# Block 1's causal attention: four projections as three fp32r products each

## The reference

```python
k, v = split(modulate(x, kv_shift, kv_scale) @ w_kv)          # 256x1024 @ 1024x2048
q = (modulate(x, shift, scale) @ wq) * 64 ** -0.5             # 16 heads of 64
s = q @ k.T - slope[h] * (t - pos), masked where pos > t
y = (softmax(s) @ v) @ wo                                     # 256x1024 @ 1024x1024
x = layer_norm(ALPHA * x + gate * y)
```

## Time and profile before

| | |
|---|---|
| Runs (us) | 2406.71, 2400.88, 2400.84; median 2400.88 |
| Profiled execution | 2402.46 us, span 2400.6 us |
| TensorE busy | 2268.5 us (94% of the span) |
| VectorE, ScalarE, GpSimd busy | 1248.1, 952.3, 113.6 us |
| DMA | 535.63 MB, 223 GB/s on average |

### The profile page before, as it was taken

How to read it: one execution, slowest core, us unless ns; L and a number is a source line. 1 busy time by engine, 2 the same in 40 slices (tenths; PEclk the granted TensorE clock), 3 DMA queues, 4 the chain that set the end, 5 groups by cost and what they waited for, 6 DMA issues and landing times.

```text
span 2400.6 us, 33267 instructions
## 1 busy us (share of the span) xinstructions
PE 2268.5 (94%) x12878; PEld 1739.5 (72%) x12878; DVE 1248.1 (52%) x2279; ACT 952.3 (40%) x1702; POOL 113.6 (5%) x96
## 2 busy tenths in 40 slices
PE   5999999998999899889999899999999998899999
PEld 3877774544576454368888689888888796698887
DVE  4724544111333411167746556777677636666776
ACT  2532212110322211165444664645545446645543
POOL 1000000000000000000024100000000052000000
PEclk8999999999999999989999899999999999999999
DMA  9966468999614899946644325466566534154663
GB/s 347 320 231 234 158 262 376 429 429 422 252 71 171 376 429 429 400 139 194 196 151 158 106 76 198 137 205 183 158 198 194 171 109 174 36 189 128 211 184 96
DMA packets 310253, 535.63 MB, mean 223 GB/s; under 512 B 14894, under 2 KB 200944, under 8 KB 296304
## 3 DMA queue, kind: packets, MB, share of 16 engines
q1 hardware_dynamic: 309180, 532.61, 61.5%
q10 hardware_dynamic: 948, 1.28, 0.2%
HBM read 532.81 MB, written 1.05 MB: 222 GB/s over the span
## 4 chain that ended last, share of the span: by engine, by line
PE 86%; DVE 7%; ACT 3%; issue 2%; DMA 2%; SPq 0%; ACTq 0%; DVEq 0%
PE bank L601 16%; PE bank L1070 14%; PE bank L892 13%; PE yacc L930 9%; PE bank L897 7%; PE bank L585 5%; PE yacc L807 2%; PE yacc L618 2%; PE bank L636 2%; PE bank L1010 1%; PE bank L1285 1%; PE yacc L1082 1%; PE bank L672 1%; PE yacc L1229 1%; PE bank L766 1%
## 5 line engine op out<-in xcount | busy, mean ns | idle before, releaser
L1449 ACT ACTIVATE arena<-bank 128x256 f32<-128x256 f32 (+3 forms) x382 | 146.6, 407 | 579.9 <-PE bank L601 127.4
L892 PE MATMUL bank<-h_split,w_hi 128*128 128x512 f32 x1408 | 351.8, 392 | 0.0
L2359 DVE TENSOR_TENSOR w_lo<-wring,w_hi 128x1024 fp32r<-128x1024 f32 x264 | 307.5, 1218 | 3.3 <-ACT w_hi L1672 3.3
L1672 ACT ACTIVATE w_hi<-wring 128x1024 fp32r<-128x1024 f32 x264 | 277.6, 1056 | 49.9 <-PE yacc L930 49.9
L892 PEld LDWEIGHTS bank<-h_split,w_hi 128*128 128x128 f32 x1408 | 259.4, 189 | 50.1
L897 PEld LDWEIGHTS bank<-h_split,w_lo 128*128 128x128 f32 x1408 | 193.6, 191 | 20.0 <-issue 4.0
L897 PE MATMUL bank<-h_split,w_lo 128*128 128x256 f32 x1408 | 201.7, 285 | 3.6 <-ACT h_split L1583 3.6
L2958 POOL TENSOR_TENSOR wx_lo<-wring,wx_hi 128x1024 fp32r<-128x1024 f32 x42 | 107.2, 2554 | 1915.5 <-ACT wx_hi L1489 1915.5
L1070 PE MATMUL bank<-arena 128*64 128x512 f32 x672 | 169.9, 599 | 12.1 <-issue 8.6
L1070 PE MATMUL bank<-wring,arena 128*64 128x512 f32 x768 | 168.9, 593 | 10.7 <-issue 6.6
L1684 ACT ACTIVATE H<-bank 128x256 f32<-128x256 f32 x176 | 67.3, 383 | 253.1 <-PE bank L897 253.1
(11 more groups left out here) (408 smaller groups left out, 3808.0 us busy)
## 6 DMA issues: line engine op xcount, KB each, us to landing
wring<-in_ffn_w_in SPq DMA_DIRECT2D x176, 512.0 KB
wring<-in_w_ada SPq DMA_DIRECT2D x24, 2048.0 KB
wring<-in_ffn_w_out SPq DMA_DIRECT2D x88, 512.0 KB
wring<-in_w_in SPq DMA_DIRECT2D x20, 2048.0 KB
wring<-in_moe_w_down SPq DMA_DIRECT2D x16, 2048.0 KB, 23.3
wring<-in_moe_w_gate SPq DMA_DIRECT2D x16, 2048.0 KB, 18.7
wring<-in_moe_w_up SPq DMA_DIRECT2D x16, 2048.0 KB, 22.2
arena<-in_moe_w_gate SPq DMA_DIRECT2D x12, 2048.0 KB, 15.1
```

Of the source, the lines that this page charges most:

```text
L892: return mm(b[:, :], r(w_hi[:, j % 2, g, c * HB:(c + 1) * HB]), r(h_split[:, c, :, :].rearrange("p a t -> p (a t)")), start=start, stop=st ...
L1449: ins = f(dst, bank_of(name)[0:dst.shape[0], 0:T] if src is None else src, func, **kw)
L1672: f(w_hi[:, j % 2, part, :].bitcast(F32R), wring[:, u % WSLOTS, part * DC * HB:(part + 1) * DC * HB], ACT.Copy).then_inc(w_hi_ready[part], 1)
L2359: tt(w_lo[:, j % 2, part, :].bitcast(F32R), wring[:, (u0 + j) % WSLOTS, part * DC * HB:(part + 1) * DC * HB], w_hi[:, j % 2, part, :], ALU ...
```

## The change

All four projections become three fp32r products. Each weight unit is cut into tiles: four tiles of two 128-row chunks by 512 columns for each `bv`, four tiles of 128 output columns for `bk` and `bq`, four 128-row chunks for `bo`, 32 tiles in all. ACT writes the high part of a tile into one of four buffers (`wb_hi`). DVE writes the low part over the raw weights in the ring (`wring_lo` is the same memory). The activations are split too: `h2_hi` and `x_hi` hold high and low of `H2`, `sq_lo` and `h_low` those of `H`, `oa_hi` (three buffers) and `oa_lo` those of the attention's output. The residual of `ln01` moves into the first eight iterations of the DVE loop. The arena's regions for the `ada` units, what their loads and the MoE 1 loads wait for, and the order of the first six MoE 1 units change.

```diff
+ADA_REGION = (0, 2, 1, 1)
+MOBA_BUFS = 4
...
+        tiles = [(f"bv{n}.{m}", f"bv{n}", 2, 512, m) for n in range(2) for m in range(4)]
...
+        def moba_freed(it):
+
+            done = [moba_q[f"bo{(it - 6) // 2}"]] if it >= 6 else []
+            done += [moba_q[f"{name}{it // 2 + 1}"] for name in ("bk", "bq") if it // 2 + 1 < DC]
+            return [q + MOBA_BUFS for q in done if q + MOBA_BUFS < len(split["moba"][1])]
...
+                    b = [fill(f"bv{n}.{i}") for i in range(TT)]
+                    for m in range(4):
+                        q = 4 * n + m
+                        hi, lo = (part_tile(part, "moba", q) for part in range(2))
+                        for p, (x, w) in enumerate(((0, hi), (1, hi), (0, lo))):
+                            if p != 1:
+                                pe.wait_ge(wt_lo_ready if p else wt_hi_ready, first + q + 1)
...
-                        product(f"{name}{m}", w[:, :, c * P:(c + 1) * P], src, fresh)
...
+                    part_product("moba", moba_q[f"bk{m}"], h2_hi, x_hi)
+                    part_product("moba", moba_q[f"bq{m}"], sq_lo, h_low, m == 0)
...
-                    w = landed(f"bo{c // 4}", 4, D)
-                    pe.wait_ge(*drained(f"moba.o{2 * c}"))
...
+                    pe.wait_ge(wt_hi_ready, first + q + 1)
+                    pe.wait_ge(wt_lo_ready, first + q + 1)
+                    pe.wait_ge(oa_low, c + 1)
...
                 elif tag == "ln01":
                     ada_turned(units[0], 0)
                     ada(units[1])
+                    for q in range(2):
+                        high("moba", q)
                 evac(f"{tag}.var", nrm[:, 0, :], func=ACT.Sqrt, scale=1.0 / D, bias=eps_ln[:, :])
...
+                        if tag == "ln01":
+                            hi = (h2_hi, sq_lo)[n][:, k, :]
+                            f(hi.bitcast(F32R), dst[:, k, :], ACT.Identity, bias=lnv[:, 2 * n + 1, k:k + 1]) \
+                                .then_inc(x_hi_ready.sem, 1)
+                            if k == DC - 1:
+                                high("moba", 2 + n)
+                            continue
...
+                            c = (it - 4) // 2
+                            evac(f"{tag}.o{it - 4}", o[:, c, :], last=False)
...
+                            evac(f"{tag}.o{it - 4}", oa_hi[:, c % 3, :].bitcast(F32R))
...
+                if it % 2 == 0:
+                    for q in moba_freed(it):
+                        high("moba", q)
...
+            def outputs_low(it):
+                if it % 2 and it >= 5:
+                    c = (it - 5) // 2
+                    dve.wait_ge(*drained(f"moba.o{2 * c}"))
+                    tt(oa_lo[:, c, :].bitcast(F32R), oa[:, c, :], oa_hi[:, c % 3, :], ALU.subtract).then_inc(oa_low, 1)
+
+            def weights_low(it):
+                if it < DC:
+                    residual_of(it)
+                if it % 2 == 0:
+                    for q in moba_freed(it - 2):
+                        low("moba", q)
...
-                          (full("moba.o14"), full("moba.o14"), (y1_summed, DC * (DC // 2)), (y1_summed, DC * (DC // 2)))]
+                          4 * [(y1_summed, DC * (DC // 2))]]
...
-                    for m in range(PAIR_UNITS):
+                    for m in (4, 0, 1, 2, 3, 5) if l and p == 0 else range(PAIR_UNITS):
...
-            sp.wait_ge(*full(f"ada{ADA_NORM['ln01'][0]}"))
+            sp.wait_ge(*full(f"ada{ADA_NORM['ln01'][2]}"))
             ada_extra(3)
```

More of the change, by code:

```diff
@@ L133, in sem @@
             return ctx.enter_context(nc.semaphore(name))
+        with nc.sbuf_tensor("wring_lo", [P, WSLOTS, WCOLS], F32) as wring_lo:
+            pass
         wring = sb("wring", [P, WSLOTS, WCOLS])
@@ L139, in build @@
         X = sb("X", [P, DC, T])
+        with nc.sbuf_tensor("h_low", [P, DC, T], F32) as h_low:
+            pass
         H = sb("H", [P, DC, T])
@@ L200, in build @@
         with ExitStack() as overlay:
+            part("before_oa", [P, 6144])
+            oa_lo, h2_hi = (part(name, [P, DC, T]) for name in ("oa_lo", "h2_hi"))
+            wb_hi = part("wb_hi", [P, MOBA_BUFS, DC * P])
+            oa_hi = part("oa_hi", [P, 3, T])
+        with ExitStack() as overlay:
             wt_mix = [part(name, [P, 2, DC * P]) for name in ("wx_hi", "wx_lo")]
@@ L426, in tile_done @@
             name, _, k, _, m = split[phase][1][q]
+            if phase == "moba" and k == 2:
+                n = q // 4
+                return (v_summed, 3 * n + m + 1) if m < 3 else full(f"bv{n}.{TT - 1}")
+            if k == 1:
+                return y1_summed, (DC // 2) * (int(name[2:]) + 1)
             if k == 2:
@@ L1187, in moba @@
             def moba():
+                first = split["moba"][0]
                 for n in range(2):
[L1190 to L1198, removed]
+                    weights(f"bv{n}", wait=False)
+                    b = [fill(f"bv{n}.{i}") for i in range(TT)]
[5 more added lines that the diff above has]
+                                pe.wait_ge(wt_lo_ready if p else wt_hi_ready, first + q + 1)
+                            for a in range(2):
+                                k = 2 * m + a
+                                if n == 0 and p < 2:
+                                    ready = x_lo_ready if p else x_hi_ready
+                                    pe.wait_ge(ready.sem, ready.upto("pe"))
+                                for i in range(TT):
+                                    last = mm(b[i][:, :], (h2_hi, x_hi)[x][:, k, i * P:(i + 1) * P].bitcast(F32R),
+                                              w[:, a, :].bitcast(F32R), start=(k == p == 0), stop=(k == DC - 1 and p == 2))
+                                    if k == DC - 1 and p == 2:
+                                        filled(f"bv{n}.{i}", last)
+                        if m < 3:
+                            last.then_inc(v_summed, 1)
                     used_by(f"bv{n}.{TT - 1}")
@@ L2424, in swiglu, with attention @@
                     step(turns, j, min(2, rest - 1 - j))
-            def attention(tag, heads, score):
+            def attention(tag, heads, score, scored=None, after=None):
                 for i in range(2):
```

109 lines of the change are left out of this document (80 added, 29 removed).

## The result

The changed kernel takes 2408.27 us, the kernel before 2402.63, medians of 13 runs each that took turns. The ratio is 1.0021 with a 95% interval of 1.0014 to 1.0028: 5 us (3.4 to 6.7) slower. That is inside the 0.3% that I called no change, but its interval excludes both no change and the 5.4 us gained that I forecast. The profiled execution took 2405.06 us with a span of 2403.3, the fastest of its 13 runs.

What follows compares the result with a forecast made beforehand. TensorE (PE) was taken to bound the attention, DMA not. 25.6 us saved less 20.2 lost left 5.4: profiled execution 2402.46 to 2397.1, or 2395.5 us as median. The range was 2383 to 2409.

Steps and rivals of the forecast that it cites:

- What PE saves: Attention's products on PE: projects save 12.9 us, out_sums 7.2, V units 5.5, together 25.6 if nothing waits.
- The norm: Norm ahead of V: two high tiles before ACT's table load make it end 1.55 us late.
- V's fourth tile: V product: the fourth high tile comes behind the pass over H, so PE waits 5.0 us.
- The clock: Behind the V tile's gap: 3 us at 0.53 of the clock, 1.5 us lost.
- rival 4: Loop: clock drops behind some ten small gaps cost 15 us, about 2410.5 us in all; chance 0.18.
- Odd iterations: Loop: out_sum waits 0.67 us for `oa_low` in iterations 5 to 13, 3.4 in all, and 2.9 in 15.
- Even iterations: Loop iterations 8, 10 and 12: first product waits 1.3 us for DVE's low tile, 3.9 in all.
- bq1 and the end: Iteration 4: ACT's wait for `bq1`'s load costs PE 1.1 us; an extra move and DVE's operation before the last out_sum, 0.85.
- Edits at nothing: Moving the residual into iterations 0 to 7, and MoE 1's changed load waits and order, cost nothing.
- The handing on: MoE 1: PE's first gate product releases the second round of loads, so a shift of PE shifts it all.
- rival 3: DMA-bound MoE 1 keeps its loads' own time and gives back the attention's gain: 2400.9 us; chance 0.07.
- Rivals 1 and 2: Waits absent except norm and end, about 2378 us, chance 0.10; loop's waits absent, V's stays, about 2384, chance 0.15.

Runs made afterwards that it cites:

- first experiment: Changed kernel with the first V weights' two high tiles behind the norm's square root, their low tiles inside the first feature pass: 2408.27 us, ratio 1.0020 to before.
- the second profile: Profile of the changed kernel with MoE 1's first six units and modulation loads in their old order: 2407.80 us, ratio 1.0023 to before.
- the best version: Changed kernel with V's tiles and modulation moves early, output low before scores, weight lows in odd iterations, `bq1`-dependent highs in iteration 5, residual late: 2386.69 us, ratio 0.9937.

## Why the prediction was wrong

The waits were right, in place and nearly in size. Two terms failed: what PE saves was put 5.8 us too high, and the clock was priced at one drop where there are three or four. Together they turned 5.4 us gained into 5 lost.

1. **What PE saves: mis-sized, 19.8 instead of 25.6.** I took an fp32r product of 24 matmuls of 256 columns at 2.75, from groups 0.915 apart. Here groups are 0.95 apart and a product takes 2.95, in every K and Q project: 7.10 to 5.89 saves 1.21, not 1.61, times 8 is 9.7. An out_sum takes 3.09, saves 0.56, not 0.90, times 8 is 4.5. V is right: 13.97 to 11.15, 5.6. This term alone eats the forecast's 5.4. Why such a matmul takes 0.119 here and 0.114 in the earlier trace rows at the same granted clock stays open.
2. **The norm: right.** 1.55 forecast, 1.50 measured: V starts 8.49 us behind the start of ACT's squares before the change and 9.99 after it (the first number of each line is the start; V's first matmul is at 614.10 before):

```profile
605.61 2.77 ACT L1559 ACTIVATE SQ<-X 128x256 f32<-128x256 f32 x8 [3.94 <-DVE X L2178]
...
605.08 2.77 ACT L1612 ACTIVATE SQ<-X 128x256 f32<-128x256 f32 x8 [3.94 <-DVE X L2253]
...
615.07 2.04 PE L1247 MATMUL bank<-wb_hi,h_hi 128*128 128x512 f32 x4 [2.57 <-ACT h_hi L1638]
```

   The table load takes 1.28, right behind the second high tile. But ahead of the fourth tile this time is worth nothing (first experiment).
3. **V's fourth tile: right.** 5.0 forecast, 4.83 measured in the second profile (2.1 in the first, where the half clock ahead of it took the rest). What I missed is that ACT's moves of the modulation stood behind the same passes: taking the tile's wait away alone gains nothing.
4. **The clock: the other step that failed.** I priced one drop, 1.5 us. There are three in one profile and four in the other: at V (2.6 where it falls behind the wait: 12 matmuls in 5.4 us from 628.38 on, for 2.8), in iteration 2 (1.5: by the starts of its matmuls the project takes 7.39 for 5.84), in iteration 15 (2.2: from 755.77 to the next turn 5.26, for 3.02 at full clock) and, in one, behind `bq1` (1.4). The experiment with the idle time filled gets 3.6 back by the medians. So rival 4 was partly true: not ten drops behind small gaps, but three or four, each behind 1.5 us and more. Not every such gap has one: in the first profile 2.1 idle us ahead of V's fourth tile and 1.6 ahead of the turn at 751.93 have none.
5. **Odd iterations: right.** 0.67 forecast, 0.78 measured, five times. Iteration 15: 2.9 forecast, 2.52.
6. **Even iterations: right.** 1.3 forecast, 1.07, 1.00 and 1.00 measured.
7. **bq1 and the end: right.** 1.1 forecast for `bq1`, 1.1 and 1.55 in the two profiles, without the clock behind it. 0.85 for the end; the last out_sum waits 1.3 where it waited 0.56, so 0.75.
8. **Edits at nothing.** The MoE 1 order: right. The handing on: right: in the best version the attention is 15.0 us shorter than before and the kernel 15.1 faster, so rival 3 is out. The residual: right in the changed kernel, as its waits show none; once DVE is fuller it costs 1.6 us of waits by the traces.
9. **Rivals 1 and 2** (the waits are not there, or half) are out: each wait of the forecast is there at nearly its size.

The terms again with measured sizes: 19.8 saved; lost 1.5 for the norm, 4.8 + 2.6 at V, 3.9 and 2.5 for `oa_lo`, 3.1 for K's low tiles, 1.1 for `bq1`, 1.5 and 2.2 for the clock, 0.8 for the end, together 24.0. That is 4.2 us slower, or 5.6 with the drop behind `bq1`; the interval is 3.4 to 6.7. These terms come from two profiles. Within one they do not close so well: in the first, where V loses 5.6 in all, they give 2.4 us, and from the start of the norm's squares to the next norm's column sums it takes 3.8 longer than before. What the other 1.4 are stays open.

## What to carry to other kernels

Splitting an operand moves PE's work to in-order queues that were never timed for it: before the split, write down for each new tile what stands ahead of it on its engine, since here the same split cost 5 us in one order and gained 15 in another. Change one thing in a kernel that is to tell what a part is worth: the plain output product came with a new order of the tiles, and the order did most of it. Size a cheaper instruction in the stage where it will stand; 4% in the pitch of a small matmul, and as much or more between products, took 5.8 us of a forecast 25.6. And ask of an idle stretch of PE (here of 1.3 us and more) for two prices, its own and that of the half clock that can follow it; when one such wait is removed, look for what stood in its shadow before counting the gain.

## What the runs showed of the hardware

- The granted clock does not fall behind every idle stretch, and the length alone does not tell: behind 1.94 us it fell and behind 1.95 it did not, at the same place of two kernels that differ only in the residual; behind 1.33 us it fell once, and not in the kernel before (752.66). The turn of iteration 2 waits 1.7 us for DVE in every profile where it isn't filled, also before the change. Before, and in the three kernels that mend V, its moves and the loop, PE ran on at 1.00 (in these three the split project took 5.86); in ten others that project took 7.05 to 7.39, in one 6.65.
- Where the clock falls differs between executions of the same attention: at 615 in one profile, at 628 and 692 in the other, 3.8 us apart over the attention (at 662 or 664 and in iteration 15 in both). The 13 times of the changed kernel lie at 2405.1 to 2406.5 and at 2408.3 to 2410.2 with none between; that this is why was argued, not shown.
- 27 idle matmuls in V's waits and 8 in iteration 2 made the kernel 3.6 us faster (+1.4 against +5.0, each against before).
